# Key-query products of a matrix memory: three products of high and low parts in place of one plain fp32 product

## The reference

```python
qk_m = silu(causal_conv(qk_m, conv_w, conv_b))     # 1024 channels: queries and keys
qm, km = split(qk_m, 2)
...
q, k, v = ch(q), ch(k) * (E ** -0.5), ch(v)
d_w = exp(d_log - m_t[..., None])                  # decay weights, causal
s_qk = einsum('bhcte,bhcse->bhcts', q, k) * d_w    # keys times queries
num = e_w * einsum(c_prev, q) + einsum('bhcts,bhcsd->bhctd', s_qk, v)
den = e_w * einsum(n_prev, q) + sum(s_qk)
h = num / maximum(abs(den), exp(-m_t))
```

## Time and profile before

| | |
|---|---|
| median of 3 runs | 1108.22 us (1107.38 to 1108.4) |
| the profiled execution | 1107.58 us |
| its span, first to last instruction | 1105.6 us |
| TensorE busy | 1096.1 us, 99% |
| VectorE busy | 785.7 us, 71% |
| ScalarE busy | 540.0 us, 49% |
| mean granted TensorE clock | 0.999 of full speed |

### The profile page before, as it was taken

One profiled execution on the slowest core, in us unless ns is written; L12 is line 12 of the kernel. 1 busy time (PEld: TensorE's weight loads), 2 busy tenths in 40 slices (PEclk: granted clock), 3 DMA queues, 4 the chain that ended last, 5 costly groups with the idle time before them and its releaser, 6 DMA issues.

```text
span 1105.6 us, 18346 instructions
## 1 busy us (share of the span) xinstructions
PE 1096.1 (99%) x6922; PEld 980.4 (89%) x6922; DVE 785.7 (71%) x1292; ACT 540.0 (49%) x933; POOL 34.5 (3%) x50
## 2 busy tenths in 40 slices
PE   9999999999999999999999999999999999999997
PEld 7999999988888888888898888889999999988886
DVE  6999999843347689774894865548999999963326
ACT  7555555643325577543463554435465555552322
POOL 0010000000002011010000000000000000000000
PEclk9999999999999999999999999999999999999999
DMA  6344343352223122242244252141233333363202
GB/s 228 99 142 146 132 134 115 132 178 95 95 63 110 58 86 86 96 152 76 76 160 127 72 177 66 49 133 58 77 115 115 115 114 102 111 203 102 95 19 76
DMA packets 33595, 121.30 MB, mean 110 GB/s; under 512 B 3900, under 2 KB 3916, under 8 KB 33264
## 3 DMA queue, kind: packets, MB, share of 16 engines
q1 hardware_dynamic: 30528, 109.07, 30.5%
q0 software_dynamic: 2992, 11.19, 2.9%
HBM read 118.13 MB, written 2.11 MB: 109 GB/s over the span
## 4 chain that ended last, share of the span: by engine, by line
PE 94%; DVE 3%; DMA 1%; issue 1%; ACT 0%; DVEq 0%; SPq 0%
PE ps L548 19%; PE ps L549 19%; PE ps L550 19%; PE ps L630 11%; PE ps L632 11%; PE ps L631 11%; DMA raw<-in_units 1%; PE ps L571 1%; PE ps L833 1%; PE ps L854 1%; PE ps L921 1%; PE ps L905 1%; PE ps L826 0%; PE ps L825 0%; PE ps L1017 0%
## 5 line engine op out<-in xcount | busy, mean ns | idle before, releaser
L1615 DVE TENSOR_TENSOR wlo<-raw,whi 128x1024 fp32r<-128x1024 f32 x115 | 142.3, 1242 | 158.3 <-ACT whi L1083 157.2
L1083 ACT ACTIVATE whi<-raw 128x1024 fp32r<-128x1024 f32 (+1 forms) x127 | 130.2, 1032 | 134.9 <-PE ps L550 124.0
L548 PE MATMUL ps<-whi,hhi 128*128 128x512 f32 x480 | 187.8, 391 | 0.0
L550 PE MATMUL ps<-whi,hlo 128*128 128x512 f32 x480 | 186.9, 389 | 0.0
L549 PE MATMUL ps<-wlo,hhi 128*128 128x512 f32 x480 | 186.8, 389 | 0.0
L548 PE MATMUL ps<-xth,whi 128*128 128x512 f32 (+1 forms) x340 | 122.4, 360 | 0.0
L549 PE MATMUL ps<-xtl,whi 128*128 128x512 f32 (+1 forms) x340 | 120.2, 354 | 0.0
L550 PEld LDWEIGHTS ps<-whi,hlo 128*128 128x128 f32 x480 | 90.1, 188 | 18.9
L548 PEld LDWEIGHTS ps<-whi,hhi 128*128 128x128 f32 x480 | 90.1, 188 | 18.5 <-ACT km L1083 0.3
L549 PEld LDWEIGHTS ps<-wlo,hhi 128*128 128x128 f32 x480 | 90.2, 188 | 18.0
L550 PE MATMUL ps<-xth,wlo 128*128 128x512 f32 (+1 forms) x260 | 98.2, 378 | 0.0
(11 more groups left out here) (261 smaller groups left out, 2739.8 us busy)
## 6 DMA issues: line engine op xcount, KB each, us to landing
raw<-in_units SPq DMA_DIRECT2D x204, 512.0 KB, 3.6
xn<-in_x POOLq DMA_DIRECT2D x4, 512.0 KB, 5.2
gb<-in_ln_g POOLq DMA_DIRECT2D x4, 512.0 KB, 3.8
gb<-in_ln_b POOLq DMA_DIRECT2D x4, 512.0 KB, 5.2
wb<-in_bias_by_key POOLq DMA_DIRECT2D x8, 256.0 KB, 3.8
out<-xn SPq DMA_DIRECT2D x8, 256.0 KB, 2.1
gsp<-g_rows POOLq DMA_DIRECT2D x1, 1024.0 KB, 4.9
memn<-in_mem_cols POOLq DMA_DIRECT2D x1, 1024.0 KB, 6.1
```

Source lines behind the costliest of these rows:

```text
L548: mm(dst, lh, rh, start=start, stop=False)
L550: return mm(dst, ll, rh, start=False, stop=stop)
L1083: return nc.scalar.activation(*a, **k)
L1615: v.tensor_tensor(low_of(c)[:, :], raw[c % RAW][:, :], whi[ring(c)][:, :].bitcast(F32), ALU.subtract).then_inc(lo_done, 1)
```

## The change

Silu's result is no longer written to `qk`. VectorE multiplies in place (into `cy`), copies the result into an F32R tile `qkh`, and subtracts that from the result into `qkl`. `kq` then multiplies by `three`. `qkh` keeps the ring of four at the same place; the low parts lie in the space of the attention's head tiles and of its values, so silu(2) also waits until the attention's last product with the values is done (`pv_done`).

```diff
-        qk = [at(f"qk{s}", [P, S], ar + (16 + 2 * s) * KB) for s in range(4)]
+        qkh = [at(f"qkh{s}", [P, S], ar + (16 + 2 * s) * KB, F32R) for s in range(4)]
+        qkl = [at(f"qkl{t}", [P, S], ar + (24 + 2 * t if t < 2 else 8 + 2 * ((t - 2) % 4)) * KB, F32R)
+               for t in range(2 * MH)]
...
-                mm(ps[j % 2][:, 0:S - j * P], qk[(2 * h + 1) % 4][:, j * P:(j + 1) * P],
-                   qk[(2 * h) % 4][:, j * P:S], start=True, stop=True).then_inc(kq_done, 1)
+                q, k, rows = 2 * h, 2 * h + 1, slice(j * P, (j + 1) * P)
+                three(ps[j % 2][:, 0:S - j * P], qkh[k % 4][:, rows], qkl[k][:, rows],
+                      qkh[q % 4][:, j * P:S], qkl[q][:, j * P:S], True, True).then_inc(kq_done, 1)
...
-                v.scalar_tensor_tensor(out=qk[t % 4][:, :], in0=e, scalar=1.0, in1=y[:, :],
-                                       op0=ALU.add, op1=ALU.mult).then_inc(conv_out, 1)
+                if t == 2:
+                    dve.wait_ge(pv_done, 2 * AH)
+                step.link(v.scalar_tensor_tensor(out=y[:, :], in0=e, scalar=1.0, in1=y[:, :],
+                                                 op0=ALU.add, op1=ALU.mult))
+                step.link(v.tensor_copy(qkh[t % 4][:, :], y[:, :]))
+                v.tensor_tensor(qkl[t][:, :], y[:, :], qkh[t % 4][:, :].bitcast(F32), ALU.subtract)\
+                    .then_inc(conv_out, 1)
```

## The result

The changed kernel takes 1110.25 us (median of 13 runs, 1109.75 to 1112.12), the kernel before 1107.51 (13 runs, 1107.09 to 1108.4). The ratio is 1.0026, with a 95% interval of 1.0019 to 1.0033: slower by 2.7 us, and more likely beyond 0.2% than within it. The forecast was 1110.0, +1.8 us. That the time was met so closely is luck: the first three runs of the kernel before lay 0.7 us above what ten more showed, and the forecast change was 0.9 us too small, and the two errors nearly cancel.

What follows compares the result with a forecast made beforehand. TensorE, busy 99%, was taken to bound the kernel. VectorE's late silus made kq(3,0) +2.45 us late, less 0.36 and 0.27, giving +1.8 us: 1109.4 on the profiled execution, 1110.0 for the median, range 1107.9 to 1111.6.

Steps and rivals of the forecast that it cites:

- the idle time ahead of weigh(2,0): VectorE's queue before head 2: 0.42 us idle plus 0.08, used up by silu(4) and (5), which grow 1.83.
- the slack ahead of head 3: Between silu(7)'s end and kq(3,0): 0.52 us, against +1.18 each from silu(6) and silu(7).
- the two instructions named: TensorE waits for weigh in head 2, about 1.7 us, and for the new subtraction ahead of head 3, about 2.
- The gain of a head: Key-query products on TensorE: 2.20 us a head falls to 1.84, a gain of 0.36 (0.29 to 0.44).
- The tail of head 2: From weigh(2,0) to head 2's numerators: 1.43 us in place of 1.75, counted as -0.05 in the sum.
- The release and head 3: kq(3,0) starts 2.45 us late, including +0.05 restart; then -0.36 for shorter products and -0.27 for ScalarE's evacuation wait.
- The copy: Silu's copy into the rounded tile on VectorE: 427 ns by one precedent, 0.46 us with its wait.
- Rival 1: Silu's copy on VectorE is slow, 0.68 us: +1.0 over four silus, 1111.1 us; chance 0.20.
- rival 2: All of VectorE's new work is hidden, only TensorE's gain counts: -1.7 us, 1106.5; chance 0.12.
- rival 4: Links between silu's instructions on VectorE cost nothing: 1109.1 us; chance 0.04.
- Rival 3, the clock,: TensorE's clock falls from 2.4 to 1.2 GHz after the second stall: +6.9 us, 1115; chance 0.04.
- the clock is below full after 545 us: Listed sign that the prediction is wrong: TensorE's granted clock not full after 545 us.

Runs made afterwards that it cites:

- e4: Split silus and three-product form for heads 0 and 1 only, the rest as in the kernel before; 0.9995 to before, stage -0.47 us.
- e1: VectorE's part alone: silus split as in the changed kernel, low parts unused, products plain fp32; 1.0040 to before, stage +3.59 us.
- e6: Changed kernel with VectorE reordered: gated(1)'s statistics and weight splits moved later, conv(7) ahead of silu(6); 1.0009 to before, stage +0.31 us.
- e5: Changed kernel with idle products in both TensorE waits, seven in head 2 and eight ahead of kq(3,0); 1.0027 to before, stage +2.88 us.
- e11: Changed kernel with ScalarE's mem_hi(1) and a small copy moved in front of weights(2,2); one run, stage 86.61 us, +4.40 against before.
- e3: Changed kernel with seven unused 512-column products in head 2's wait, between kq(2,1) and kq(2,2); 1.0034 to before, stage +2.88 us.
- e9: Heads 0 to 2 as in the changed kernel, silu(6), silu(7) and head 3 as before; 1.0015 to before, stage +1.21 us.
- e10: e9 with seven unused products in head 2's wait; 1.0009 to before, stage +1.20 us.
- e2: TensorE's part alone: one-instruction silu writes the rounded tile, three products read it as both parts; 0.9997 to before, stage -0.49 us.
- e9b: e9 unchanged, run again for a second profile; one run, stage 84.60 us, +2.39 against the kernel before.
- e9c: e9 unchanged, run again for a third profile; one run, stage 84.50 us, +2.29 against the kernel before.

## Why the prediction was right, and which terms were mis-sized

The mechanism that makes the loss was right at each step, though not what it said of the clock (below): heads 0 and 1 hide their silus (e4), the new work of silu(4) and (5) uses up the idle time ahead of weigh(2,0), that of silu(6) and (7) the slack ahead of head 3, and TensorE waits twice, for the two instructions named. e1 and e4 together show it, and e6 shows that the place, not the amount, costs. The change was forecast at +1.8 and is +2.9 in the stage; three terms make nearly all of the difference of 1.06 (all taken from the start of kq(0,0)):

- **The gain of a head**, "0.36 us a head (0.29 to 0.44)", is 0.24. The 512 and 384 products save 0.27, not 0.33 (before, 479.90 to the second product behind them at 481.69; after, 479.45 to 480.97), and the 256 and 128 ones cost 0.03 more than the passes that they replace (0.88 before, 0.91 after, measured alike). Conv(5) is 0.48 early and not 0.72, weigh(2,0) 0.85 late and not 0.61: +0.24. The value lay outside my own bounds, since I had compared pieces of the chain one by one and not the distance between the neighbours of the whole group.
- **The tail of head 2**, "takes 1.43 from weigh(2,0) in place of 1.75": weigh(2,2) starts 1.86 behind weigh(2,0), where it was 1.51. I had -0.05 and it was +0.35: +0.40.
- **The release and head 3**: "+0.05 restart" is 0.04 of latency and another 0.27 because a released product takes 0.50 in the chain (e5). With 0.12 less gain in head 3 than counted this is +0.38. The wait for ScalarE's key tile did disappear, as said.
- The remaining 0.04 is of the size of the rounding between the two views.

**The copy** was sized by its single precedent, and rightly: 427 ns, eight times. Rival 1 did not occur, nor did rival 2 (e1) and rival 4: the linked multiply-add is followed after 0.72 us, not 0.60. The Trainium skill ("VectorE: DVE Perf Modes", The DRAIN you can't avoid) has the semaphore for nothing, measured with copies. The trace of the changed kernel does not agree for these instructions: 0.72 us behind the waited-for multiply-add, 0.61 behind the subtraction, which is as long and is not waited for.

**Rival 3, the clock,** was real where I had looked for it least: behind the first wait, in whose wake a longer wait hid it. It had been priced at +5.1 behind the second wait; behind that one it costs 1.5 (e11), for the clock returns before the work that I had doubled is over. The prediction had also named "the clock is below full after 545 us" as a sign of being wrong, and this sign came: 0.57 from 546 to 550. That the time was met all the same is luck in this step. The fall lay where the second wait hid it, and made that wait 0.8 us in place of 2.1. Whether other executions of the changed kernel have the fall behind the second wait, as e11's has (which differs by nothing that would slow TensorE), was not shown. A long execution is no proof of it: the changed kernel's times go up to 1112.12, but e5's profiled execution took 1111.47 with the full clock and a stage of 85.09, and had lost its time ahead of the stage.

**Open:** why weigh(2,2) comes 0.27 to 0.35 us later whenever weigh(2,0) starts straight behind VectorE's own work. It does so in the changed kernel, e1, e3, e5, the three profiles of e9, e10 and e11 (1.86 us), and not in before, e4 (1.51), e2 and e6 (1.59). The clock (e3), the form of the product (e1) and ScalarE's idle time (e11) are excluded. The records do tell where the time goes. Weigh(2,2) needs the product and the decay weights, and VectorE's sequencer stands at an instruction of its own that waits for the weights. Its times in the stretch 543 to 547, shortest, median and longest in ns, before and then changed:

```profile
L2040 DVEq EVENT_SEMAPHORE  x3: 50/208/806, 544.4 to 545.9; - x3
```

```profile
L2048 DVEq EVENT_SEMAPHORE  x4: 50/50/2431, 543.0 to 546.7; - x4
```

The longest of each is the one ahead of weigh(2,2), and it ends 1.46 us behind the start of weigh(2,0) in both kernels. So the inputs are not later. But weigh(2,2) starts 0.05 us behind this end in the kernel before and 0.40 behind it in the changed one, and the same 0.05 and 0.40 divide all the profiles: 0.05 where the sequencer had stood there for 0.8 to 1.0 us, 0.40 where it had stood for 2.1 to 2.4. Whether the length of the wait is the cause was not tested.

## What to carry to other kernels

Before work is moved to an engine with a low busy share, follow that engine's own queue to each instruction that the bounding engine waits for, and compare the added time with the idle time ahead of that one instruction: here 9.4 us of added work cost nothing in its first half and 2.9 us in its second. Moving 2.4 us of patient work behind the release, with conv(7) ahead of silu(6), gave back 2.6 in the stage. Patient is not the same as free: 0.6 of it was lost again 18 us later, where TensorE waited for splits that now came late (e6), so the whole span is to be compared and not the stage alone. A narrow fp32 product gains nothing from the three-product form (0.27 us at 512 and 384 columns, -0.03 at 256 and 128), so the change looks worth making only for wide ones whose split is hidden (a kernel with the wide ones alone was not run), and here even heads 0 and 1 (-0.5 us of 1107) are below what the times can tell. A gain is also lost where the next thing waits for a third engine (e2's head 3).

## What the runs showed of the hardware

- A product of 512 columns that is released by a wait takes 0.50 us from start to end, where its record in a stream is 0.39, and the next one starts 0.33 to 0.34 us behind it in place of 0.23. Products of no use up to 0.24 us before the release do not change it (e5).
- Behind a wait of 1.8 us, TensorE's clock fell from 2.4 to 1.2 GHz for some 3.4 us in the changed kernel, in e9b and in e9c. It did not in e9's first profile, the same program, whose stage is 1.1 to 1.2 us shorter. It did not fall behind the first waits of e11 and e1 either, nor behind the second waits of e1 and e3 (2.3 us each), and it did behind e11's second (2.3 us). So the length of the wait alone does not decide it.
- With seven products of no use in the first wait it stayed full there in the profiles of e3, e5 and e10, where three of six profiles without them have the fall. e10's eleven executions are within 1.3 us of one another where e9's spread over 2.6. That these products keep the clock up is likely from this, and not certain.
- The Trainium skill ("TensorE: Matmul & The Clock Gate", What's actually happening) says that the moment at which the clock rises at a kernel's start varies from run to run. e9, e9b and e9c show more than that: whether it falls at all in mid-kernel differs between executions of one program.
- Where a fall lies ahead of a longer wait for another engine, it costs nothing (e3 against the changed kernel, both 85.09).
- VectorE's weigh(2,2) starts 0.05 or 0.40 us after its sequencer's wait has ended, in all thirteen profiles one or the other (see Open).
